# First unit's routing moved ahead of the output projection's last product in a one-core PEER transformer layer

## What is computed

```python
y_x = jnp.concatenate([fourier_branch(proj_x, w_fmix), y_x_ssm], axis=-1) @ w_out
x = x + gm_x * rms_norm(y_x, g_post_mix)
hx2 = modulate(rms_norm(x, g_pre_ffn), sf_x, cf_x)
# peer_ffn, for each block tb of 128 tokens:
q = (tb @ w_query).reshape(tbn, 8, 128)
s1 = jnp.einsum('thd,hkd->thk', q[..., :64], sub_keys_1)     # 128 keys
s2 = jnp.einsum('thd,hkd->thk', q[..., 64:], sub_keys_2)
v1, i1 = lax.top_k(s1, 16)
v2, i2 = lax.top_k(s2, 16)                                    # 16 x 16 sums, top 16 of these
gate = softmax(top_s)
act = gelu(einsum('td,thkd->thk', tb, expert_u[idx]))
out = einsum('thk,thkd->td', gate * act, expert_v[idx])
```

## Time and profile before

| | |
|---|---|
| runs (median) | 1841.42 us |
| profiled execution, whole | 1850.07 us |
| its span | 1848.2 us, granted clock 0.883 |
| TensorE matmul busy | 1459.7 us (79%) |
| VectorE | 1316.4 us (71%) |
| ScalarE | 434.9 us (24%) |
| GpSimd (POOL) | 888.9 us (48%) |
| a dot (L1378), x256 | 2288 ns each |
| DMA over the span | 683.72 MB, mean 370 GB/s |
| software queue q0 (POOL) | 503.36 MB, 67.8% of 16 engines' span |
| hardware queue q1 (SP) | 176.36 MB, 25.3% |

### The profile page before, as it was taken

How to read it: one execution, slowest core, us unless ns; L and a number is a source line. 1 busy time by engine, 2 the same in 40 slices (tenths; PEclk the granted TensorE clock), 3 DMA queues, 4 the chain that set the end, 5 groups by cost and what they waited for, 6 DMA issues and landing times.

```text
span 1848.2 us, 13641 instructions
## 1 busy us (share of the span) xinstructions
PE 1459.7 (79%) x4521; PEld 708.2 (38%) x4521; DVE 1316.4 (71%) x1684; ACT 434.9 (24%) x1160; POOL 888.9 (48%) x666
## 2 busy tenths in 40 slices
PE   5999999999999655555566566669999999989920
PEld 3434464556449511111112233345444444433310
DVE  3127888665328999999998787988565666556689
ACT  3012212121113212212122576787100000000000
POOL 0012243211104788888777777746455554322273
PEclk9999999999999776676666998979999999999975
DMA  9998997885749999999999999979999999999997
GB/s 361 374 347 329 344 358 259 314 330 212 280 136 354 353 419 419 419 419 418 419 419 417 406 407 377 389 307 375 408 413 413 413 414 413 376 418 417 417 421 315
DMA packets 164021, 683.72 MB, mean 370 GB/s; under 512 B 16432, under 2 KB 19056, under 8 KB 120688
## 3 DMA queue, kind: packets, MB, share of 16 engines
q0 software_dynamic: 92160, 503.36, 67.8%
q1 hardware_dynamic: 71360, 176.36, 25.3%
q10 hardware_dynamic: 432, 3.15, 0.4%
HBM read 678.51 MB, written 4.29 MB: 369 GB/s over the span
## 4 chain that ended last, share of the span: by engine, by line
DMA 34%; PE 29%; DVE 16%; POOL 14%; issue 5%; SPq 1%; ACT 0%; DVEq 0%; POOLq 0%; ACTq 0%
DMA arena<-in_expert_v,arena 26%; POOL arena L568 14%; DMA arena<-in_expert_u,arena 7%; PE PS L1662 6%; PE PS L1803 6%; PE PS L1563 5%; DVE arena L1378 5%; PE PS L1544 3%; DVE arena L1421 3%; PE PS L1879 2%; DVE arena L1413 2%; PE PS L1519 1%; DMA arena<-in_w_in 1%; PE PS L1686 1%; SPq L384 1%
## 5 line engine op out<-in xcount | busy, mean ns | idle before, releaser
L1378 DVE CUSTOM_DVE_ANT_0 arena<-arena 128x2048 f32<-128x2048 f32 x256 | 578.4, 2288 | 95.7 <-DMA arena<-in_expert_u,arena 93.5
L1879 PE MATMUL PS<-arena 128*128 128x512 f32 x512 | 356.1, 833 | 251.9 <-DMA arena<-in_expert_v,arena 246.9
L568 POOL DMA_INDIRECT arena<-in_expert_v,arena x256 | 402.4, 1572 | 284.7 <-DVE arena L1421 111.5
L568 POOL DMA_INDIRECT arena<-in_expert_u,arena x256 | 389.7, 1522 | 262.2 <-DVE arena L1378 94.1
L1931 PE MATMUL PS<-arena 128*128 128x512 f32 x1024 | 453.0, 600 | 19.5 <-DMA arena<-in_expert_v 17.7
L1931 PEld LDWEIGHTS PS<-arena 128*128 128x128 f32 x1024 | 193.1, 191 | 278.7 <-issue 232.5
L1879 PEld LDWEIGHTS PS<-arena 128*128 128x128 f32 x512 | 114.4, 247 | 461.7 <-DMA arena<-in_expert_v,arena 363.0
L1421 DVE SCALAR_TENSOR_TENSOR arena<-arena 128x2048 f32<-128x2048 f32 x62 | 145.8, 2351 | 58.1 <-DMA arena<-in_expert_v,arena 56.0
L1097 DVE SCALAR_TENSOR_TENSOR arena<-arena 128x1024 f32<-128x1024 f32 x120 | 160.8, 1340 | 21.8 <-DMA arena<-in_w_mod 18.9
L498 POOL DMA_DIRECT2D arena<-in_w_mod x128 | 68.5, 537 | 220.6 <-DVE arena L1097 190.8
L951 ACT ACTIVATE arena<-arena 128x4 f32<-128x4 f32 x64 | 13.0, 203 | 587.4 <-DVE arena L1378 515.3
(11 more groups left out here) (247 smaller groups left out, 1342.6 us busy)
## 6 DMA issues: line engine op xcount, KB each, us to landing
arena<-in_w_mod POOLq DMA_DIRECT2D x128, 512.0 KB, 6.7
arena<-in_expert_v SPq DMA_DIRECT2D x128, 512.0 KB
arena<-in_w_mod SPq DMA_DIRECT2D x32, 1024.0 KB, 14.4
arena<-in_w_in SPq DMA_DIRECT2D x28, 1024.0 KB, 14.5
arena<-in_w_out SPq DMA_DIRECT2D x16, 1024.0 KB, 12.9
arena<-in_w_query SPq DMA_DIRECT2D x8, 1024.0 KB, 8.5
arena<-in_x SPq DMA_DIRECT2D x4, 1024.0 KB, 6.3
arena<-cum_rows SPq DMA_DIRECT2D x4, 1024.0 KB, 9.6
```

Source lines behind the costliest of these rows:

```text
L568: nc.gpsimd.indirect_dma_start(slot, None, table, bass.IndirectOffsetOnAxis(ap=rows[:, n:n + 1], axis=0),).then_inc(arrived, 16)
L1378: V.tensor_tensor_reduce(out=rows, in0=rows, in1=h2row[u // PH], scale=1.0, scalar=0.0, op0=ALU.mult, op1=ALU.add, accum_out=dots[:, u % B ...
L1879: ins = M(PS[:, b, :], diag_slot[m % DIAGS], slot[:, b * NQ:(b + 1) * NQ], start=(m == 0), stop=(m == BLK - 1))
```

## The change

Unit 0's transposes, query and key scores are issued on TensorE between (2,1) and (3,1), and ScalarE's copies of them between those of the same two products. For that the transposes of block 0 go to PSUM banks 4 to 7 instead of 0 to 3, and unit 0's q and scores to places of their own. Head 0's 128 query columns are read once more, to `first_query`, by a load of 1 MB behind the load of quarter 2 of `w_out` on SP; the two halves of `w_query` are still read whole. On VectorE `pick_keys(0)` and `pick_pairs(0)` come ahead of `x1_make(1)`, and `x1_variance(1)` and `h2_make(1)` behind the dot of row 1.

```diff
+SECOND_ROW_AFTER = 1
...
+        first_query = at(191, 2048).rearrange("p (k n) -> p k n", k=KT)
+        first_qT, first_scores = at(179, P), at(178, 256)
...
 # SP
-            for j in range(R_OUT + 2, R_QUERY):
-                ring_load(j)
+            ring_load(R_OUT + 2)
+            sp.wait_ge(y_ps, 2)
+            sp.dma_start(first_query, w_query.rearrange("(k p) n -> p k n", p=P)[:, :, 0:P]).then_inc(mid_in, 16)
+            ring_load(R_OUT + 3)
...
 # ScalarE
             for n, t in OUT_ORDER:
...
+                if (n, t) == (2, 1):
+                    h2T_out(0)
+                    q_out(0)
+                    scores_out(0)
             y_norm(1)
...
-            h2T_out(0)
-            for u in range(UNITS):
-                t, h = divmod(u, PH)
-                act.wait_ge(q_ps, u + 1)
-                A(qT[:, h, t * P:(t + 1) * P], PS[:, 4 + u % 2, 0:P], ACT.Copy).then_inc(q_evac, 1)
-                if u != 1:
-                    scores_out(max(u - 1, 0))
-                if u == 0:
+            for u in range(1, UNITS):
+                q_out(u)
+                if u == 1:
                     x1_norm(1)
+                else:
+                    scores_out(u - 1)
...
 # VectorE
             x1_make(0)
             x1_variance(0)
             h2_make(0)
-            x1_make(1)
...
             pick_keys(0)
-            x1_variance(1)
             pick_pairs(0)
-            h2_make(1)
+            x1_make(1)
             for n in range(N_DENSE):
                 dot(n)
+                if n == SECOND_ROW_AFTER:
+                    x1_variance(1)
+                    h2_make(1)
...
 # TensorE
             for n, t in OUT_ORDER:
...
+                if (n, t) == (2, 1):
+                    h2_transposes(0)
+                    query(0)
+                    pe.wait_ge(keys_in, 32)
+                    key_scores(0)
+
+            for u in range(1, UNITS):
                 query(u)
-                if u == 0:
-                    pe.wait_ge(keys_in, 32)
-                if u != 1:
-
-                    key_scores(max(u - 1, 0))
+                if u > 1:
+                    key_scores(u - 1)
                 if u == H2T_AT:
                     h2_transposes(1)
             key_scores(UNITS - 1)
```

More of the change, by code:

```diff
@@ L828, in x1_norm, with h2T_out, q_out, scores_out @@
                 A(xsq[:, t:t + 1], xsq[:, t:t + 1], ACT.Sqrt).then_inc(std_ready, 1)
+            def h2T_out(t):
+                for q in range(4):
+                    act.wait_ge(h2T_ps, 4 * t + q + 1)
+                    A(h2T[t][:, 4 * q:4 * q + 4, :], PS[:, 4 - 4 * t + q, :].rearrange("p (k t) -> p k t", k=4),
+                      ACT.Copy).then_inc(h2T_evac, 1)
+            def q_out(u):
+                t, h = divmod(u, PH)
+                act.wait_ge(q_ps, u + 1)
+                A(qT[:, h, t * P:(t + 1) * P] if u else first_qT, PS[:, 4 + u % 2, 0:P], ACT.Copy).then_inc(q_evac, 1)
+            def scores_out(u):
+                act.wait_ge(sc_ps, u + 1)
+                if u == 1:
+                    act.wait_ge(x1_ready, 2)
+                if u == PH:
+                    act.wait_ge(h2_ready, 2)
+                A(scores[u // PH][:, u % PH, :] if u else first_scores, PS[:, 6 + u % 2, 0:256], ACT.Copy).then_inc(sc_evac, 1)
             act.wait_ge(yt_ps, 2)
@@ L1331, in pick_keys @@
                 for a in range(2):
-                    top16(v12[:, a, :], i12[:, a, :], scores[u // PH][:, u % PH, a * NKEYS:(a + 1) * NKEYS], s_cut)
+                    top16(v12[:, a, :], i12[:, a, :], (scores[u // PH][:, u % PH] if u else first_scores)[:, a * NKEYS:(a + 1) * NKEYS], s_cut)
                 go(V.tensor_copy(i12f, i12))
@@ L1805, in w_out, with h2_transposes, query, key_scores @@
                 return ins
+            def h2_transposes(t):
+                pe.wait_ge(h2_ready, t + 1)
+                for q in range(4):
+                    if t:
+                        pe.wait_ge(wo_evac, OUT_ORDER.index((2 + q // 2, q % 2)) + 1)
+                    elif q == 0:
+                        pe.wait_ge(rows_evac, 2)
+                    for i in range(4):
+                        k = 4 * q + i
+                        ins = nc.tensor.transpose(PS[:, 4 - 4 * t + q, i * P:(i + 1) * P], h2row[t][:, k * P:(k + 1) * P], ident)
+                    ins.then_inc(h2T_ps, 1)
+            def query(u):
+                t, h = divmod(u, PH)
+                j = R_QUERY + h // 4
+                if u:
+                    ring_wait(j)
+                else:
+                    pe.wait_ge(mid_in, 48)
+                if u >= 2:
+                    pe.wait_ge(q_evac, u - 1)
+                for k in range(KT):
+                    if h == 0 and k % 4 == 0:
+                        pe.wait_ge(h2T_evac, 4 * t + k // 4 + 1)
+                    ins = M(PS[:, 4 + u % 2, 0:P], wring[j % 2][:, k, (h % 4) * P:(h % 4 + 1) * P] if u else first_query[:, k, :], h2T[t][:, k, :],
+                            start=(k == 0), stop=(k == KT - 1))
+                ins.then_inc(q_ps, 1)
+            def key_scores(u):
+                t, h = divmod(u, PH)
+                pe.wait_ge(q_evac, u + 1)
+                if u >= 2:
+                    pe.wait_ge(sc_evac, u - 1)
+                M(PS[:, 6 + u % 2, 0:256], qT[:, h, t * P:(t + 1) * P] if u else first_qT, keys[:, h, :], start=True, stop=True).then_inc(sc_ps, 1)
             for n, t in OUT_ORDER:
```

## The result

| | before | after |
|---|---|---|
| median of the runs made side by side | 1841.76 us | 1848.06 us |
| ratio (95% interval) | | 1.0046 (1.0030 to 1.0062), about +8.5 us |
| span of the profiled execution | 1848.2 us | 1845.7 us |
| TensorE / VectorE / ScalarE / POOL busy | 1459.7 / 1316.4 / 434.9 / 888.9 us | 1454.9 / 1315.6 / 435.0 / 887.5 us |

What follows compares the result with a forecast made beforehand. Gathers of expert rows saturating the DMA engines were taken as the bound; gather 20's data at 640.7 instead of 633.0 add 7.7 us: 1848.2 + 7.7 = 1855.9, less 8.65 us (profiled run to median) is 1849.1; range -2.8 to +11.2 us.

Steps and rivals of the forecast that it cites:

- Chain forward: TensorE to POOL, unit 0: query from 542.9, indices at 558.2, gather 0 at 559.0 instead of 572.6, 13.5 us earlier.
- What it pushes back: TensorE's (3,1) ends at 561.4, 7.6 us later; the query weights' second-half load and x1_make(1) wait for it.
- The collision: DMA queues from 562.9: 8.0 MB of gathers and query weights take 20 us; query 4 starts at 584.5, 11.8 us later.
- The clock: TensorE behind query 4: 5.6 us at 1.2 GHz after the stall, 2.8 us lost; query 15 ends at 636.8.
- The lead of the early slots: Gathers 4 to 19: gather 4 lands some 8 us behind issue, early slots run about 3.6 us early.
- Gather 20's data: Entry to the saturated stretch: issued at 637.7, data start 3 us behind, at 640.7 instead of 633.0, +7.7 us.
- The added load of 1 MB: Head 0's load on SP's queue: 5.0 us without cover, but hidden; nothing to 1 us, taken as nothing.
- Carried to the end: Saturated stretch behind gather 20: DMA share is 1.02, so nothing gives the +7.7 us back; chance 0.58 (+4 to +11).
- rival 1: At query 4: weights arrive in time, POOL never waits at gather 20; 3.5 us gained, 1837.9; chance 0.18.
- Rival 2: From 1200 to 1300: the stall happens but is made up later, up to all 7.7 us, 1841.4; chance 0.19.
- Rival 3: VectorE's chain: the head start of 13.5 us is carried whole and sets the end, 1827.9; chance 0.05.

Runs made afterwards that it cites:

- e5: Changed kernel with POOL waiting ahead of gather 0 until the second half of the query weights has landed; ratio to the kernel before 1.0076, +14.0 us.
- e4: Changed kernel with unit 1's exponentials on ScalarE issued behind unit 11's scores instead of behind the last scores; ratio to the kernel before 1.0017, +3.1 us.
- e1: The kernel before, no edit, traced a second time; gathers 160 to 195 took 140.5 us, against 145.5 in its first trace and 140.2 in the changed kernel.
- e7: Changed kernel with second-half query weights loaded in pieces, gathers 2 and 3 held until they land, unit 1's exponentials earlier; ratio to the kernel before 0.9966, -6.3 us.
- e2: Changed kernel with the second half of the query weights loaded in four pieces, each once its slot quarter is read; ratio to the kernel before 0.9998, -0.4 us.

## Why the prediction was right, step by step

The forecast was 1849.1, that is 1.0042 as ratio to 1841.42; measured are 1.0046. All times here are put on the origin of the trace before (+2.90).

- **Chain forward**: gather 0 was forecast for 559.0 and went at 558.6. TensorE's wait for h2 was 0.66 us, forecast 0.6. Right.
- **What it pushes back**: the weights' issue 561.15 (forecast 561.4), x1_make(1) through at 568.0 (568.3). Right.
- **The collision**: query 4 at 584.2, forecast 584.5. The total was right because both queues together move a fixed amount. The share was wrong: I weighed the turns by bytes and set strict turns of an 8 KB row against a 2 KB row aside, and the trace after shows just these, 92 packets against 92. What I held against them does not hold: the 5 us of the earlier trace rows with rows of 4 KB against 2 KB contain a stretch in which the software queue had little to send (23 packets against 170 from 472 to 473); where both were busy in the trace before, it is one for one there too (70 packets against 73 from 474 to 475). The Trainium skill, DMA: Bandwidth & Descriptors, section Queues, rings and completion order, has the engines take the queues in turn by packets; the trace agrees (337 packets against 324 from 562 to 570). The weights did not land at 588 for it, for two reasons. POOL issued the four gathers in 0.9 to 1.0 us each, faster than the 2.5 and 2.0 us of gathers 0 and 1 before, so that all but a few of their packets were out of the way by 571 of the trace after. And gather 4, issued at 575.00, took no turn from the weights: the software queue moved nothing from 575 to 581. One term of the sum was too small by itself: the weights' data started 3.7 us behind their issue (nothing on the hardware queue from 558 to 561.5, the first packet at 562.0), not 1.5. e5, where the weights come alone and first, shows the stall by way of ScalarE.
- **The clock**: I took 2.8 us; query 4 lost 5.37 - 3.73 = 1.6 us and the next ran at full speed. The fall was forecast right, its price was not.
- **The lead of the early slots**: forecast 3.6 us, measured 0.9 (gather 10 at 596.45 + 2.90 against 600.25). Wrong: gather 4 landed 12.3 us behind its issue, not 8. Its data start 6.5 us behind the issue, while the hardware queue held the engines at 98%.
- **Gather 20's data**: forecast at 640.7, that is +7.7 us; they start near 634.4 + 2.90 = 637.3, +4.3 us. The query chain was shorter (clock), and from issue to data it took 1.6 us and not 3: POOL's instruction took 0.93 us here and 2.46 at gather 0 before. The term was mis-sized by nearly half.
- **A term left out**: VectorE's wait of 10.5 us at unit 1's weights. I had looked at `pick_keys(2)`, two dots further on, and not at ScalarE's program, in which the exponentials stand behind the last scores. The second hole goes with it, 2.5 us in the bytes and at gather 100, and e4, in which that hole is gone, shows what the first alone gives: +4.0 at gather 100, which fits the +4.3 just named. So the forecast has the mechanism right (late weights, late queries, late gather 20, DMA engines without work), and its size came out by two errors that nearly cancel: 3.4 us too many in the first hole, and 2.5 for the second, which it did not have. That part is luck. What the second hole is worth at the end of the kernel is open (e4).
- **The added load of 1 MB**: forecast nothing, and nothing is seen (the 2.90 us above are the same on both sides of it).
- **Carried to the end**: right, as e1 shows. Over the kernels of the table gather 100's delay and the measured time agree within 2 us, wherever the delay came from, where each time is known to about 3 us; I had argued it from the saturated DMA engines.
- **The rivals**: rival 1 (the weights in time) is what e7 builds: it gains 6.3 us where 3.5 were given. The price was low because gather 4's dot, forecast to end at 589.7, ends 49.2 us behind the origin in e7 (49.3 in e2), which is 587.6: the early slots lead by 5.8 us at gather 10, not by 3.6. Rival 2 fell with e1. Rival 3's 13.5 us are not there in any kernel; e7 has the head start whole and keeps 5 to 6 us.

## What to carry to other kernels

When work is put ahead of a step, list the transfers that wait for that step's end to get their buffer: what cost time here was 7.6 us of TensorE work and behind it a 4 MB load, pushed out of an idle stretch of the DMA engines and in among the gathers that the change itself had made early. Such a load can often be cut so that each piece waits only for the reads of its own part of the buffer; here that alone turned +0.46% into nothing, and with two gathers held back for the load the reordering gained 0.3%. Then follow each engine's program from the step that comes late to every wait on it: the same late query was waited for on POOL and, through ScalarE's order of instructions, on VectorE; with that wait taken away in e4, VectorE waited for it one step further on. At last ask what the late engine's work will coincide with when it resumes: here dots fell on the gathers that should have filled the DMA engines.

## What the runs showed of the hardware that I had not expected

With rows of 8 KB gathered on the software queue and rows of 2 KB on the hardware queue, both full, the engines served one packet of each in turn (92 and 92 in 2 us), which left the hardware queue 0.19 of 0.85 MB. With rows of 4 KB against 2 KB it is the same in the kernel before, from 474 to 475:

```profile
q0 software_dynamic: 70, 0.26, 64.2%
q1 hardware_dynamic: 73, 0.15, 37.6%
```

The counts of a longer stretch, 290 and 458 in the earlier trace rows, hide this, because one queue was not full all the time: before reading a share from two counts, see that both queues had work in each part of the stretch.

An indirect gather issued at 575.00 while the hardware queue was full began to move data only at about 581.5, and 0.13 MB had gone by 582:

```profile
q1 hardware_dynamic: 424, 1.57, 98.0%
q0 software_dynamic: 16, 0.13, 7.7%
```

(queues from 578 to 582 after.) The same instruction on quiet engines took 1.6 us (gather 20 after) to 3.2 us (gather 0 before) to its data, in both cases 0.7 us behind the end of POOL's instruction; here it was 3.8 us behind that end. It is not a matter of the software queue alone: the weights, issued at 558.25 while gathers kept the engines busy, moved their first packet 3.7 us later, against 1.0 us in the kernel before and in e5, where the engines were idle. So a queue that joins busy engines began about 3 us late both ways. Why was not tried and stays open.

How long POOL takes to issue a gather goes with what VectorE does. From 540 to 1100 us of the trace after, 89 gathers began with no dot under way (or under 0.3 us of one in their first 0.9 us): none took more than 1.02 us. Of the 162 others 146 took more than 1.1 us, 1.91 in the median. Before the change it was 3 of 86 and 148 of 166. In the saturated stretch this costs nothing, since the DMA engines have gathers waiting; behind a hole it would keep them from filling up again. No run was made to part it from other causes.
